# Routed experts on one core: gate and up products in banks of their own, and the next block's transposes in two halves around the hidden ones

## What is computed

```python
def expert_block(args):
    toks, ws, e = args
    xb = u_pad[toks]
    hid = jax.nn.silu(xb @ we_gate[e]) * (xb @ we_up[e])
    return (hid @ we_down[e]) * ws[:, None]
```

## Time and profile before

| | |
|---|---|
| median of 3 runs | 2447.31 us |
| profiled execution, its own time | 2452.52 us |
| its span | 2450.5 us |
| PE busy | 2254.6 us (92%) |
| DVE, ACT, POOL busy | 1161.1, 691.6, 667.0 us |
| mean granted clock of TensorE | 0.958 |
| HBM read | 326.19 MB |

### The profile page before, as it was taken

How to read it: one execution, slowest core, us unless ns; L and a number is a source line. 1 busy time by engine, 2 the same in 40 slices (tenths; PEclk the granted TensorE clock), 3 DMA queues, 4 the chain that set the end, 5 groups by cost and what they waited for, 6 DMA issues and landing times.

```text
span 2450.5 us, 28540 instructions
## 1 busy us (share of the span) xinstructions
PE 2254.6 (92%) x10572; PEld 1480.4 (60%) x10573; DVE 1161.1 (47%) x1754; ACT 691.6 (28%) x1092; POOL 667.0 (27%) x419
## 2 busy tenths in 40 slices
PE   6999899999989899999997898999799989988896
PEld 5887557888768666877776673476433333333333
DVE  3545665699861455888888340045511111111113
ACT  3333573333332333334433230123111011100112
POOL 2322003433343323433332131033122222222220
PEclk9999699999989989999998899999999999999998
DMA  3224002355541222222221113131679789989764
GB/s 132 87 78 138 1 2 69 128 181 192 183 146 64 77 73 87 83 69 69 69 69 52 35 35 137 69 125 59 254 255 325 242 278 311 352 315 365 255 184 129
DMA packets 163726, 353.72 MB, mean 144 GB/s; under 512 B 9457, under 2 KB 100593, under 8 KB 145457
## 3 DMA queue, kind: packets, MB, share of 16 engines
q1 hardware_dynamic: 146352, 297.18, 34.2%
q0 software_dynamic: 16128, 51.06, 8.7%
q10 hardware_dynamic: 1152, 4.19, 0.4%
HBM read 326.19 MB, written 34.60 MB: 147 GB/s over the span
## 4 chain that ended last, share of the span: by engine, by line
PE 76%; DMA 9%; DVE 8%; ACT 3%; issue 2%; POOL 1%; SPq 0%; POOLq 0%; ACTq 0%; DVEq 0%
PE bank L772 26%; PE bank L1371 11%; PE bank L1103 7%; PE bank L763 7%; PE bank L1392 6%; DMA arena<-in_we_up 4%; PE bank L1017 3%; DMA arena<-in_we_down 2%; PE bank L1350 2%; PE bank L898 1%; PE bank L781 1%; PE bank L1142 1%; DMA arena<-in_w_up 1%; PE bank L782 1%; DVE arena L2118 1%
## 5 line engine op out<-in xcount | busy, mean ns | idle before, releaser
L1371 PE MATMUL bank<-arena,hn 128*64 128x512 f32 x1536 | 344.3, 601 | 28.3 <-DMA arena<-in_we_up 27.7
L674 POOL TENSOR_TENSOR w_low_flat<-arena,in_high 128x1024 fp32r<-128x1024 f32 (+1 forms) x73 | 184.3, 2546 | 386.9 <-ACT in_high L1681 386.8
L1371 PEld LDWEIGHTS bank<-arena,hn 128*64 128x64 f32 x1536 | 117.2, 139 | 248.2 <-issue 247.1
L1392 PE MATMUL bank<-arena 128*64 128x512 f32 x768 | 175.4, 598 | 28.5 <-DVE arena L2532 27.3
L2527 DVE TENSOR_TENSOR inv<-inv,bank 128x256 f32<-128x256 f32 x48 | 20.2, 421 | 365.6 <-ACT inv L1903 365.6
L1903 ACT ACTIVATE inv<-bank 128x256 f32<-128x256 f32 x48 | 18.4, 383 | 554.2 <-PE bank L1371 554.2
L763 PE MATMUL bank<-arena 128*128 128x512 f32 x320 | 142.6, 605 | 6.7 <-DMA arena<-in_w_br_ssd 6.7
L658 POOL TENSOR_TENSOR w_low<-arena,w_high 128x2048 fp32r<-128x2048 f32 x22 | 103.3, 4696 | 160.1 <-ACT w_high L1597 160.1
L2539 DVE SCALAR_TENSOR_TENSOR sq<-bank,arena 128x512 f32<-128x512 f32 x96 | 72.1, 751 | 147.7 <-PE bank L1392 147.7
L1103 PE MATMUL bank<-in_x,in_high 128*128 128x512 f32 x336 | 135.4, 403 | 0.0
L772 PE MATMUL bank<-x_high,w_high 128*128 128x512 f32 x336 | 133.5, 397 | 1.1 <-POOL w_low L658 1.1
(11 more groups left out here) (451 smaller groups left out, 4786.8 us busy)
## 6 DMA issues: line engine op xcount, KB each, us to landing
arena<-in_we_gate SPq DMA_DIRECT2D x47, 1024.0 KB
arena<-in_we_up SPq DMA_DIRECT2D x47, 1024.0 KB
arena<-in_we_down SPq DMA_DIRECT2D x47, 1024.0 KB, 7.6
arena<-in_w_in SPq DMA_DIRECT2D x40, 1024.0 KB, 5.3
arena<-in_w_ada SPq DMA_DIRECT2D x12, 2048.0 KB, 8.0
arena<-in_w_up SPq DMA_DIRECT2D x22, 1024.0 KB, 10.8
arena<-in_w_in SPq DMA_DIRECT2D x18, 512.0 KB, 4.7
arena<-in_w_out SPq DMA_DIRECT2D x4, 2048.0 KB, 7.9
```

The costliest lines, as they stand in the source:

```text
L674: pool_eng.tensor_tensor(in2_tile(j, "low"), in2_tile(j, "whole"), in2_tile(j, "high").bitcast(f32), ALU.subtract).then_inc(S("w_low"), 1)
L1371: ins = nc.tensor.matmul(rows_of(out, c), columns_of(moe["xT"][:, p, :], k, c), gate_up[:, :, k, :], start=k == 0, stop=k == KD - 1)
L1392: ins = nc.tensor.matmul(rows_of(banks[5 + half], c), columns_of(moe["hidT"][:, p, :], k, c), moe["dn"][:, 2 * p + c, at:at + 512], start= ...
```

## The change

`block_up` goes through all gate matmuls (256 columns, bank 2) and then all up matmuls (256 columns, bank 3). It waits for the gate weights ahead of the first and for the up weights ahead of the second. The banks no longer alternate between blocks. A new semaphore `moe_gate` is raised at the end of the gate part, and ACT's `block_gate` waits for it. `up_through` is raised at the end of the up part, as before; DVE's `block_hidden` now waits for it beside `moe_sg`. `block_transposes` gets a half, and the order in a block becomes up, first half, hidden transposes, second half, down.

```diff
-            def block_transposes(b, p, gathers):
-
-                pe.wait_ge(S(f"x_gathered{p}"), gathers * 16)
-                for half in range(2):
-                    for q in range(4):
-                        c = (4 * half + q) * P
-                        ins = nc.tensor.transpose(banks[half][:, q * P:(q + 1) * P], moe["X"][:, p, c:c + P], ident)
-                    ins.then_inc(S("moe_tr"), 1)
+            def block_transposes(b, p, gathers, half):
+
+                if half == 0:
+                    pe.wait_ge(S(f"x_gathered{p}"), gathers * 16)
+                for q in range(4):
+                    c = (4 * half + q) * P
+                    ins = nc.tensor.transpose(banks[half][:, q * P:(q + 1) * P], moe["X"][:, p, c:c + P], ident)
+                ins.then_inc(S("moe_tr"), 1)
...
             def block_up(b, p):
+
                 needed = loads_needed(b)
                 pe.wait_ge(S("xT_done"), b * 2 + 2)
-                for name in ("we_gate", "we_up"):
+                for part, name in enumerate(("we_gate", "we_up")):
                     pe.wait_ge(S(f"{name}_in"), needed)
-                out = banks[2 + p].rearrange("p (t n) -> p t n", n=FE)
-                for k in range(KD):
-                    for c in range(2):
-                        gate_up = moe["gu"][:, 2 * p + c, :].rearrange("p (t k n) -> p t k n", t=2, n=FE)
-                        ins = nc.tensor.matmul(rows_of(out, c), columns_of(moe["xT"][:, p, :], k, c), gate_up[:, :, k, :],
-                                               start=k == 0, stop=k == KD - 1)
-                ins.then_inc(S("up_through"), 1)
+                    for k in range(KD):
+                        for c in range(2):
+                            at = (part * KD + k) * FE
+                            ins = nc.tensor.matmul(rows_of(banks[2 + part][:, 0:FE], c), columns_of(moe["xT"][:, p, :], k, c),
+                                                   moe["gu"][:, 2 * p + c, at:at + FE], start=k == 0, stop=k == KD - 1)
+                    ins.then_inc(S(("moe_gate", "up_through")[part]), 1)
...
+            def block(b, p, gathers):
+
+                block_up(b, p)
+                block_transposes(b + 1, 1 - p, gathers, 0)
+                hidden_transposes(b, p)
+                block_transposes(b + 1, 1 - p, gathers, 1)
+                block_down(b, p)
...
             def block_gate(b, p):
-                act.wait_ge(S("up_through"), b + 3)
-                nc.scalar.activation(moe["sg"][:, p, :], banks[2 + p][:, 0:FE], ACT.Silu).then_inc(S("moe_sg"), 1)
+                act.wait_ge(S("moe_gate"), b + 1)
+                nc.scalar.activation(moe["sg"][:, p, :], banks[2][:, 0:FE], ACT.Silu).then_inc(S("moe_sg"), 1)
...
             def block_hidden(b, p):
                 dve.wait_ge(S("moe_sg"), b + 1)
-                nc.vector.tensor_tensor(moe["hid"][:, p, :], moe["sg"][:, p, :], banks[2 + p][:, FE:2 * FE], ALU.mult)\
+                dve.wait_ge(S("up_through"), b + 3)
+                nc.vector.tensor_tensor(moe["hid"][:, p, :], moe["sg"][:, p, :], banks[3][:, 0:FE], ALU.mult)\
                   .then_inc(S("moe_hid"), 1)
```

More of the change, by code:

```diff
@@ L1399, in _ @@
             pairs = pairs_but_one + 1
[L1400 to L1404, removed]
+            def block(b, p, gathers):
[4 more added lines that the diff above has]
+                block_down(b, p)
+            for half in range(2):
+                block_transposes(0, 0, 1, half)
+            block(0, 0, 1)
             with pe.Fori(1, pairs) as i:
                 for b, p in ((i * 2 + (-1), 1), (i * 2, 0)):
[L1409 to L1412, removed]
+                    block(b, p, i + 1)
             block_up(pairs_but_one * 2 + 1, 1)
```

## The result

The change runs in 2429.82 us (median of 5 runs, 2428.14 to 2432.92), the kernel before in 2447.31 us (5 runs, 2446.22 to 2455.72) beside it. The ratio is 0.9915, 95% interval 0.990 to 0.993, so 20.8 us faster by the ratio (17 to 24) and 17.5 by the medians. The profiled execution took 2429.97 us with a span of 2427.8. From the first up matmul of block 0 to the end of the last down matmul the expert loop took 638.1 us before (1775.63 to 2413.76) and takes 617.0 now (1773.36 to 2390.38), 21.1 less; nearly all of the gain is there. The profiled execution of before was 5.2 us above the median of its runs, so its loop is read somewhat long.

The account below looks back on a forecast made before the run. The prediction took PE to bound most expert blocks and weight transfers the clusters. 33 blocks at 0.42 us (13.9) plus 8.0 and 1.9 at the clusters gave 23.8 us off 2447.3: 2423.5 us, range 2413 to 2436.

Parts of the forecast that it names:

- The gate's place: With E the up matmuls' end, hidden transposes start at E+0.52 instead of E+0.94: 0.42 us gained per block.
- Doubling the matmuls at 0: In the up part, twice as many 256-column matmuls and weight loads over the same columns add 0 us.
- The second half of the transposes at 0: Placed behind the hidden transposes, it fits inside the 1.09 us until the DVE copy is back, so costs nothing.
- The clusters: Groups of blocks waiting for weights gain by starting on gate weights before up weights land: 8.0 + 1.9 us.
- The 2.7 us that were to be kept: At clusters' last waits, gate weights land 2.7 us before up weights, so the up part ends 2.7 us earlier.
- DMA takes the cluster part: Rival: in the clusters landings come later by what PE gained; 13.9 us is left, 2433.4 us; chance 0.16.
- The clusters dissolve: Rival: short waits for weights vanish and stretched up parts go; 32 us faster, 2415.4 us; chance 0.11.
- Added loads show: Rival: 32 added weight loads per block in the up part are not hidden, 1.7 us per block, 2505 us; chance 0.04.
- It does nothing: Rival: hidden transposes still start as the eighth transpose ends, or the stage is all DMA; 2447 us; chance 0.03.

Follow-up runs that it names:

- gate_first: The change without splitting the transposes: gate first in its own bank, all eight transposes before the hidden ones; 2436.76 us, 0.9948 of the kernel before.
- narrow: The kernel before with up matmuls of 256 columns, all gate then all up, same bank, no wait moved; 2450.64 us, ratio 1.0004.
- halves_only: The kernel before with only the transposes split in halves, gate and up still in one bank; 2447.06 us, ratio 1.0001.
- both_waits: The change, but PE waits for gate and up weights ahead of the first gate matmul; 2442.02 us, 0.9966 of the kernel before.
- gate_freed: The change, but a lane's next gate load waits only for the gate part's end; 2430.35 us, 0.9919 of the kernel before.
- sp_early: The change, with SP reading the next run's numbers ahead of the previous run's down load; 2432.47 us, 0.9931 of the kernel before.
- sp_early_freed: sp_early with gate loads that wait only for the gate part's end; 2430.56 us, 0.9927 of the kernel before.

## Why the prediction was right, point by point

**The forecast.** 23.8 us faster was predicted, 20.8 by the ratio and 17.5 by the medians were measured; the profiled executions differ by 22.6. The range (2413 to 2436) holds it. The case is the forecast's in the sum: blocks gain between up and down, clusters gain a part.

**The gate's place** held to the hundredth: product at E + 0.04, hidden transposes at E + 0.52, first down matmul at E + 1.62 (1.61 predicted). That is 0.41 of the 0.42. One reading behind it was wrong: before, the eight transposes did not hold the hidden ones to E + 0.94. DVE's product did, and without it they could start at E + 0.76 (gate_first). So of the 0.41 the gate alone gives 0.17 and the split on top of it 0.24.

**Doubling the matmuls at 0** was the term that was mis-sized: 0.04 us per block, 2 us in all, shown by narrow. The block gains 0.37 in the end. The price of a load that shows was a rival's, 1.7 us per block. The sentence of the Trainium skill (TensorE: Matmul & The Clock Gate, Part 3: Packing small matmuls) that a weight load overlaps a running matmul only where row groups differ does not agree with these runs: all loads use all rows, and twice as many cost 0.04 us.

**The second half of the transposes at 0** held; their cover is the DVE copy. It is shown too that neither part of the change alone gives the 0.4: in halves_only the gate and the product hold the hidden transposes, in gate_first PE still stands idle 0.60 us for the copy behind them. The 0.14 of gate_first was not foreseen.

**The clusters** were put at 9.9 us (8.0 + 1.9) beside 33 blocks. The loop's 21.1 less 33 x 0.37 = 12.2 leaves 8.9. That figure is soft: halves_only has the block and the time of before, and a loop of 634.6; against it 5.4 are left. Added up over all blocks, 48 x 0.37 = 17.8 and 7.1 of waits (27.7 to 20.6), less 4.2 by which the stretched up parts grew (4.6 to 8.8), make 20.7 of the 21.1.

The sum came near, its parts did not. Each row below runs from the start of one up part to that of another, in both timelines. It ends one block behind a cluster's last wait, so the forecast has a block's 0.42 beside what it put on the waits:

| stretch of the kernel before | us before | us after | gained | forecast | gained against halves_only |
|---|---|---|---|---|---|
| 1927.68 to 2007.83, 6 blocks | 80.15 | 80.25 | -0.1 | 3.1 | 0.3 |
| 2083.16 to 2123.64, 3 blocks | 40.48 | 36.94 | 3.5 | 1.4 | 2.0 |
| 2123.64 to 2185.20, 4 blocks | 61.56 | 60.74 | 0.8 | 3.1 | 1.5 |
| 2197.76 to 2288.04, 6 blocks | 90.28 | 83.88 | 6.4 | 4.0 | 3.1 |

The 2.7 us that were to be kept at 1995.24 and at 2170.84 were not. At the first, the block's start had gained 2.2 us within the stretch, and then it ran 9.75 us in place of 7.09 at the lower clock; in the other cluster the block at 2140.31 was stretched to 9.78, where its like before took 7.09. I had let the clock stand as it was. That the other two stretches gave more than forecast is luck, and differs between executions. What the clusters would have given without the stretching is not shown, since a block inside a cluster that ends sooner may only wait longer for the next landing. That PE's start on the gate weights alone is what the clusters gain by is shown by both_waits; that issuing loads earlier gives nothing more is shown by gate_freed and sp_early.

**The rivals.** "DMA takes the cluster part" is refuted by both_waits, though its mechanism, full DMA engines, fits the failure of gate_freed, sp_early and sp_early_freed. "The clusters dissolve" did not come: six waits are left, and more stretching, not less. "Added loads show" has its price measured, 0.04 in place of 1.7 us. "It does nothing" fell with the first block.

**Open.** Which wait brings the slow clock is not settled. In the profiles here every wait for weights of 4.1 us or more was followed by a stretched up part, but some of 2.6 to 3.9 us were too (2.57 in both_waits) and others of 3.4 to 3.7 were not the earlier trace rows. Keeping PE busy in the waits was not tried.

## What to carry to other kernels

Before splitting work around a wait, ask which engine ends the wait: moving PE's transposes changed nothing until ACT's work had moved off the path, and both together were worth more than either. Where a pipeline waited for several transfers that share a full DMA, issuing them earlier gave nothing here, but starting on the one that had landed did. Count also what PE pays after standing idle: up parts at a lower granted clock cost 4.2 us more than before, against 7.1 less of waiting. And compare starts from one view: a step of the chain begins where the step before it ends, a row of the timeline where the instruction does.

## What was not expected of the hardware

From the weight load of the two hidden transposes to the start of DVE's copy it is 0.54 or 0.55 us in all 48 blocks of before, of the change and of gate_first, whether DVE's product had just released them or they followed eight transposes without a gap. In gate_first their weights were loaded (from E + 0.76) while the transposes in front still ran (to E + 1.02). And 64 matmul records of 256 columns with 64 weight loads ran in 6.91 us against 6.87 for 32 of 512, so each of the 32 added loads of 64 columns, with a matmul of 256 columns to hide behind, cost about 0.001 us.
